# A float32 two-block transformer: last attention product, routing and experts joined in one block, routing by pairs of tiles

## The chip, the cores and the metric

The kernel runs on one core of a Trainium2 chip. The metric is the time of one execution in microseconds (us).

## The reference

512 tokens of width 1024 in float32 pass through a first model (pooling mixer, latent attention, two SwiGLU layers, a final norm) and then through a second block. Of the second block, what matters here is its end:

```
x = x + diff_attention(rmsnorm(x, norm_mix))        # its last step: o @ w_out
h = rmsnorm(x, norm_ffn)
logit_g = h @ w_group + b_group                     # 4 groups
g_sel   = argmax(logit_g);  gate_g = softmax(logit_g)[g_sel]
logit_e = (h @ w_router + b_router)[g_sel]          # the 4 experts of that group
top_v, top_i = top_k(softmax(logit_e), 2);  top_v = top_v / sum(top_v)
x = x + sum over the two experts e of gate_g * top_v[e] *
        (silu(h @ w_gate[e]) * (h @ w_up[e])) @ w_down[e]     # 16 experts, inner width 512
```

## The kernel before

X holds the 512 tokens as 4 tiles of 128 tokens on the partitions. Every large product is made as three matmuls of reduced-precision halves: `product` (L248 to L252) takes a high and a low half of both operands. The halves are made on the way: ScalarE (ACT) writes the high half, VectorE (DVE) subtracts it from the original. Weights stream in units of 128 x 2048 floats (1 MB), in the first part through `raw`, WH, WL, in the experts through `eraw` (8 slots), WEH, WEL (4 slots each).

`da_out` is the last attention product. PE turns the four tiles of heads (L1793), then makes 16 `unit_into` calls: 4 weight units times 4 tiles, each 12 matmuls with 512 columns. DVE adds each finished tile to X (L1884), ACT sums its squares into the junk space `da_flat` (L571). Then `recycle()` frees the semaphores behind a barrier of all engines, the memory of the attention is given back, and `run_experts` opens a new block. Only there do the loads of the first 8 expert units start (`prefetch`, L2171), because `eraw` lies where the attention's tiles were.

`route` follows in the order written out: root and reciprocal of the four sums (L265, L272); DVE makes the normed rows of all tiles with the gain (`rows_g`, L2037), PE turns them (L1962), ACT and DVE split them into halves (L2003, L2046), PE makes logits for all 512 tokens (24 matmuls of 512 columns), DVE copies them, PE turns them back (L1974). A chain of small DVE instructions then finds the group and the two experts by maxima and first matches (L2054 to L2076). PE counts how many earlier tokens chose each expert (`ranked`, L1979 and L1982), DVE works out a slot for each token and writes one-hot rows (L2086 to L2107), PE turns these into two tables, token and share of each slot, with 8 float32 matmuls (L1989). ACT copies the shares out, DVE the indices. SP, the queue that issues plain loads and stores, stores the normed rows in `moe_rows` and X in `out` meanwhile (L1951 to L1954), with the second four expert units behind them.

Then a loop runs over rounds of at most 128 tokens per expert (one round with these inputs) and inside it over the 16 experts. POOL gathers 128 rows of `moe_rows` by index (L2410, L2414), PE turns them (L2210), ACT and DVE split them (L2281, L2344), PE makes gate, up and down products from 6 units per expert, DVE making each unit's low half (L2339) after ACT's high half (L2277). ACT scales the result by the share (L2298), and POOL adds it to the rows of `out` (L2425). Each new expert unit is requested by SP when DVE is done with the unit in its slot (L2192). Gathered rows lie in X's first two tiles, results in its last two, so the loop may not start before X is stored.

## Time and profile before

| | us |
|---|---|
| median of three runs (lowest, highest) | 1587.02 (1586.5, 1595.58) |
| the profiled execution: its time, its span | 1586.74, 1584.7 |
| last attention product, from its first product matmul to the last, on the span's clock | 1186.7 to 1230.5 |
| first expert matmul | 1279.1 |
| ACT's scaling of the last expert's result | 1573.2 |

All starts are microseconds from the start of the span. The span is what the profiler saw of the program; the execution's own time is 2.0 us longer. PE is TensorE, PEld its loads of stationary operands, DVE VectorE, ACT ScalarE, POOL GpSimd, SPq the DMA issues of SyncE. A fp32 matmul whose operands are not in the reduced type leaves two records per instruction, a fp32 transpose one.

### The profile page before, as it was taken

To read this page: it belongs to the slowest core of one execution; us is meant where nothing else is said; L and a number is where in the kernel's file an instruction comes from. 1 tells how busy PE (TensorE), PEld (TensorE's weight loads), DVE (VectorE), ACT (ScalarE), POOL (GpSimd) and SP (SyncE) were. 2 spreads that over 40 slices of the span, in tenths; PEclk is the share of its full clock that TensorE was granted. 3 is DMA by queue.
4 is the path that set the end of the run, shared out by engine and by line. 5 is a ranking of instruction groups with operands and counts; after the bars stand their busy time and mean duration, and the time that the engine had idled before them with its cause. 6 is when DMAs were issued, how large, how long until landed. Compare 5 with 4: busy or idle time off the path is not lost. (4 is left out here: it accounts for less than half of the span.)

```text
span 1584.7 us, 18928 instructions
## 1 busy us (share of the span) xinstructions
PE 1505.3 (95%) x7353; PEld 1238.4 (78%) x7353; DVE 781.5 (49%) x922; ACT 674.1 (43%) x854; POOL 77.2 (5%) x57
## 2 busy tenths in 40 slices
PE   8999999999899999999999999999879479999996
PEld 7888888888787788888888887888558368888885
DVE  6432333222575334333332226344872578888884
ACT  5322222211356433322221125434861267777783
POOL 0000000000000000000000000000220012211110
PEclk9999999999999999999999999999989789999998
DMA  6222223223130112223233231322000889999993
GB/s 240 77 83 106 102 83 106 93 94 115 59 128 6 57 65 106 79 106 106 79 106 107 80 120 53 131 99 80 27 1 1 317 306 380 384 382 383 392 390 81
DMA packets 36160, 226.19 MB, mean 143 GB/s; under 512 B 5223, under 2 KB 5479, under 8 KB 11776
## 3 DMA queue, kind: packets, MB, share of 16 engines
q1 hardware_dynamic: 31344, 212.05, 35.4%
q0 software_dynamic: 4608, 13.22, 3.6%
q8 instruction: 45, 0.74, 0.2%
q14 instruction: 19, 0.16, 0.0%
q10 hardware_dynamic: 144, 0.03, 0.0%
HBM read 215.21 MB, written 13.63 MB: 144 GB/s over the span
## 5 line engine op out<-in xcount | busy, mean ns | idle before, releaser
L245 DVE TENSOR_TENSOR WL<-raw,WH 128x2048 fp32r<-128x2048 f32 x93 | 214.0, 2301 | 432.7 <-ACT WH L240 432.7
L250 PE MATMUL PS<-AH,WL 128*128 128x512 f32 (+1 forms) x768 | 286.4, 373 | 4.3 <-DVE AL L319 4.3
L251 PE MATMUL PS<-AL,WH 128*128 128x512 f32 (+1 forms) x768 | 285.8, 372 | 0.0
L252 PE MATMUL PS<-AH,WH 128*128 128x512 f32 (+1 forms) x768 | 285.7, 372 | 0.0
L240 ACT ACTIVATE WH<-raw 128x2048 fp32r<-128x2048 f32 x93 | 177.6, 1910 | 241.1 <-PE PS L252 241.1
L2339 DVE TENSOR_TENSOR WEL<-eraw,WEH 128x2048 fp32r<-128x2048 f32 x96 | 216.7, 2287 | 17.1 <-ACT WEH L2277 17.1
L2277 ACT ACTIVATE WEH<-eraw 128x2048 fp32r<-128x2048 f32 x96 | 181.6, 1912 | 19.8 <-PE PS L252 18.8
L250 PEld LDWEIGHTS PS<-AH,WL 128*128 128x128 f32 x768 | 145.4, 189 | 29.6 <-DVE AL L319 4.5
L252 PEld LDWEIGHTS PS<-AH,WH 128*128 128x128 f32 x768 | 145.3, 189 | 25.0
L251 PEld LDWEIGHTS PS<-AL,WH 128*128 128x128 f32 x768 | 145.4, 189 | 24.9
L250 PE MATMUL PS<-WH,AL 128*128 128x512 f32 (+2 forms) x416 | 155.3, 373 | 7.7 <-DVE WL L245 7.7
L252 PE MATMUL PS<-WH,AH 128*128 128x512 f32 (+2 forms) x416 | 153.2, 368 | 0.0
L251 PE MATMUL PS<-WL,AH 128*128 128x512 f32 (+2 forms) x416 | 153.1, 368 | 0.0
L250 PE MATMUL PS<-WEH,AH 128*128 128x512 f32 x256 | 103.5, 404 | 2.5 <-DVE AH L2344 2.5
L251 PE MATMUL PS<-WEL,AH 128*128 128x512 f32 x256 | 101.9, 398 | 0.0
L252 PE MATMUL PS<-WEH,AH 128*128 128x512 f32 x256 | 101.8, 398 | 0.0
L250 PEld LDWEIGHTS PS<-WH,AL 128*128 128x128 f32 x416 | 78.9, 190 | 21.8 <-DVE WL L245 6.8
L252 PEld LDWEIGHTS PS<-WH,AH 128*128 128x128 f32 x416 | 78.9, 190 | 12.7
L251 PEld LDWEIGHTS PS<-WL,AH 128*128 128x128 f32 x416 | 79.0, 190 | 11.9
L250 PE MATMUL PS<-WH,f0FL 128*128 128x512 f32 x176 | 69.8, 396 | 0.0
L252 PE MATMUL PS<-WH,f0FH 128*128 128x512 f32 x176 | 69.6, 396 | 0.0
L251 PE MATMUL PS<-WL,f0FH 128*128 128x512 f32 x176 | 69.6, 395 | 0.0
(312 smaller groups left out, 2104.2 us busy)
## 6 DMA issues: line engine op xcount, KB each, us to landing
eraw<-experts SPq DMA_DIRECT2D x96, 1024.0 KB, 12.8
raw<-stream SPq DMA_DIRECT2D x94, 1024.0 KB, 4.8
moe_rows<-moe_rows_g SPq DMA_DIRECT2D x5, 512.0 KB, 14.4
X<-x SPq DMA_DIRECT2D x4, 512.0 KB, 4.6
out<-X SPq DMA_DIRECT2D x1, 2048.0 KB, 20.3
ffn_row<-rows SPq DMA_DIRECT2D x2, 512.0 KB, 10.0
final_row<-rows SPq DMA_DIRECT2D x2, 512.0 KB, 6.2
cst<-consts SPq DMA_DIRECT2D x1, 733.5 KB, 13.3
```

Source lines behind the costliest of these rows:

```text
L240: act.activation(WH[:, u % SLOTS, :], raw[:, u % SLOTS, :], ACT.Copy).then_inc(unit_hi, 1)
L245: dve.tensor_tensor(WL[:, u % SLOTS, :], raw[:, u % SLOTS, :], WH[:, u % SLOTS, :].bitcast(F32), ALU.subtract).then_inc(unit_lo, 1)
L250: pe.matmul(acc, lhs_lo, rhs_hi, start=start, stop=False)
L251: pe.matmul(acc, lhs_hi, rhs_lo, start=False, stop=False)
L252: return pe.matmul(acc, lhs_hi, rhs_hi, start=False, stop=stop)
L2277: act.activation(WEH[:, k % ESLOTS, :], eraw[:, k % ERAW, :], ACT.Copy).then_inc(unit_hi, 1)
L2339: dve.tensor_tensor(WEL[:, k % ESLOTS, :], eraw[:, k % ERAW, :], WEH[:, k % ESLOTS, :].bitcast(F32), ALU.subtract).then_inc(unit_lo, 1)
```

## The change

One block now holds the attention's end, the routing and the experts: the barrier and the second block are gone. Three things allow it. The memory of `eraw` is laid over the attention's QT, KT, V and probabilities (for which the output O and the scratch `half` change places), and SP requests the first four expert units once all scores are made, the other four once the last head is weighted. X itself is turned and multiplied by router weights that carry the gain; the factor 1/root of a token is applied to its 20 logits afterwards. These logits are plain float32 matmuls with the turned X as stationary operand. And the tiles are routed in two pairs: the first pair between the units of the attention product, the second behind it.

Instead of the chain of maxima, an expert's rank within its group is counted: all 4 x 4 differences of a group are compared with a tiny constant and summed. The first table holds the tokens alone, as reduced-type matmuls in two parts; the shares have a table of their own behind it, and the exponentials stand next to it. The last tile is added, gained and turned in halves. In the expert loop, DVE copies index and share of the next round at the end of a round instead of at its beginning, and splits two units, not three, before the first rows.

```diff
...
-        differential_attention(block, later, w, v, down_made, mix_row_here, mix_row, mix_rows_g)
+        scored, weighed, made, heads_lo = differential_attention(block, later, w, v, down_made, mix_row_here, mix_row,
+                                                                 mix_rows_g)
+        later.close()
+        wctx.close()
+        m = expert_memory()
+        run_experts(block, m, *route(block, m, scored, weighed, made, heads_lo))
...
-    O = flat[:, 0:T * D].rearrange("p (t d) -> p t d", t=T)
-    half = flat[:, T * D:2 * T * D].rearrange("p (m n) -> p m n", m=2)
+    O = flat[:, T * D:2 * T * D].rearrange("p (t d) -> p t d", t=T)
+    half = flat[:, 0:T * D].rearrange("p (m n) -> p m n", m=2)
...
-        square_sums(act, added, sem("do_next_summed"), O, range(T))
...
+def expert_memory():
...
+    m.told_share = m.rows_g[:, 0, 0:512].rearrange("p (k n) -> p k n", n=ROUNDS * E)
+    sb("expert_gap", [P, SLOTS * UNIT - n[0] // 4])
+    m.WEL = sb("WEL", [P, ESLOTS, UNIT], F32R)
+    m.eraw = sb("eraw", [P, ERAW, UNIT])
+    with ExitStack() as before:
+        m.XT = sb("moe_turned", [P, T, C, P], where=before)
+    m.WEH = sb("WEH", [P, ESLOTS, UNIT], F32R)
...
+def route(block, m, qk_used, weighed, made, heads_lo):
...
+        sp.wait_ge(qk_used, 2 * H * T)
+        m.prefetch(sp, 0, 4)
+        sp.wait_ge(weighed, H * T)
+        m.prefetch(sp, 4, ERAW)
...
+        x_out(0)
+        sp.dma_start(out[S:S + P, :], X[:, 0, :]).then_inc(x_stored, 16)
+        x_out(1)
+        row_out(0)
+        sp.dma_start(moe_rows[S:S + P, :], m.rows_g[:, 0, :]).then_inc(rows_stored[0], 16)
+        row_out(1)
+        x_out(2)
+        row_out(2)
+        row_out(3)
+        x_out(3)
...
+        def turn_x(t, half):
+            pe.wait_ge(added, t + 1 + (half if t == last else 0))
+            for c in range(4 * half, 4 * half + 4):
+                mm = pe.transpose(PS[:, 2 * t + half, cols(c % 4)], X[:, t, cols(c)], ident)
+            mm.then_inc(x_turned, 1)
+
+        def logits(t, half):
+            if t == last and half:
+                pe.wait_ge(copied_last, 1)
+            else:
+                pe.wait_ge(copied, t + 1)
+            for c in range(4 * half, 4 * half + 4):
+                mm = pe.matmul(PS[:, 2 * t, 0:20], m.XT[:, t, c, :], m.wr[:, c, :],
+                               start=(c == 0), stop=(c == C - 1))
+            if half:
+                mm.then_inc(logits_made, 1)
+
...
+        unit_into(3, 0).then_inc(made, 1)
+        unit_into(3, 1).then_inc(made, 1)
+        turn_x(0, 0)
+        turn_x(0, 1)
+        unit_into(2, 2)
+        turn_x(1, 0)
+        turn_x(1, 1)
+        pe.wait_ge(weighted, 1)
+        logits(0, 0)
+        logits(0, 1)
+        unit_into(3, 2).then_inc(made, 1)
+        logits(1, 0)
+        logits(1, 1)
+        unit_into(2, last).then_inc(unit_used, 1)
+        pe.wait_ge(tables, 2)
+        pe.wait_ge(selected, 2)
+        pe.matmul(PS[:, 1, 0:2 * E], m.before_r[:, :], m.both[:, 0:2, :].rearrange("p t e -> p (t e)"),
+                  start=True, stop=False)
+        pe.matmul(PS[:, 1, E:2 * E], m.ones_r[:, :], m.both[:, 0, :], start=False, stop=True).then_inc(ranked, 1)
+        turn_x(2, 0)
+        turn_x(2, 1)
+        for half in range(2):
+            for j in (6, 7):
+                mm = unit_half(3, last, j, half)
+            mm.then_inc(unit_used if half else made, 1)
+        turn_x(last, 0)
+        turn_x(last, 1)
+        for t in (2, last):
+            logits(t, 0)
+            logits(t, 1)
+        table(0)
+
+        pe.wait_ge(selected, 3)
+        pe.matmul(PS[:, 5, 0:3 * E], m.before_r[:, :], m.both[:, 2:5, :].rearrange("p t e -> p (t e)"),
...
+        table(1).then_inc(tabled, 1)
+
+        pe.wait_ge(weighted_out, 1)
+        for n in range(2 * T):
+            k, t = divmod(n, T)
+            mm = pe.matmul(PS[:, 7, 0:ROUNDS * E], ALF[:, k, cols(t)], m.told_share[:, n, :],
+                           start=(n == 0), stop=(n == 2 * T - 1))
+        mm.then_inc(shares_tabled, 1)
...
+        for t in range(last):
+            square(t)
+            act.wait_ge(summed, t + 1)
+            root(t)
+            act.wait_ge(x_turned, 2 * t + 2)
+            act.activation(m.XT[:, t, :, :], tile_banks(t), ACT.Copy).then_inc(copied, 1)
+        square_half(0)
+        act.wait_ge(x_turned, 2 * last + 1)
+        act.activation(m.XT[:, last, 0:4, :], PS[:, 2 * last, :].rearrange("p (c s) -> p c s", s=P),
+                       ACT.Copy).then_inc(copied, 1)
+        square_half(1)
+        act.wait_ge(sum_added, 1)
+        root(last)
+        act.wait_ge(scaled, 2)
+        act.wait_ge(inverted, T)
+        act.activation(m.rows_g[:, last % 2, :], m.rows_g[:, last % 2, :], ACT.Copy,
+                       scale=rstd[:, last:T]).then_inc(gained, 1)
...
+            dve.wait_ge(step, n[0])
+            then(dve.tensor_tensor(D4, fours.unsqueeze(2).broadcast_to([P, 10, 4, 4]),
+                                   fours.unsqueeze(3).broadcast_to([P, 10, 4, 4]), ALU.subtract))
+            then(dve.tensor_tensor(D16, D16, const("order").unsqueeze(1).broadcast_to([P, 10, 16]), ALU.is_ge))
+            then(dve.tensor_reduce(m.rank[:, ts, :, :].rearrange("p t g e -> p (t g) e"), D4, AX_X, ALU.add))
+            then(dve.tensor_scalar(m.group[:, ts, :], m.rank[:, ts, 0, :], 0.0, None, ALU.is_equal))
+            group = m.group[:, ts, :].unsqueeze(3).broadcast_to([P, 2, G, 4])
+            dve.scalar_tensor_tensor(m.both[:, ts, :].rearrange("p t (g e) -> p t g e", g=G), m.rank[:, ts, 1:5, :],
+                                     1.5, group, ALU.is_lt, ALU.mult).then_inc(selected, 1)
+            for k in range(2):
...
+        invert(0)
+        row(0)
+        invert(1)
+        row(1)
+        add(2)
+        logit(0)
+        logit(1)
+        select(0)
+        invert(2)
+        row(2)
+        place(0)
+        add_half(0)
+        dve.wait_ge(rows_stored[1], 16)
+        gain_half(0)
+        add_half(1)
+        gain_half(1)
+        dve.wait_ge(x_turned, 2 * T)
+        dve.tensor_copy(m.XT[:, last, 4:8, :], PS[:, 2 * last + 1, :].rearrange("p (c s) -> p c s", s=P)
+                        ).then_inc(copied_last, 1)
+        dve.wait_ge(summed, T + 1)
+        dve.tensor_tensor(rstd[:, last:T], m.halves[:, 0:1], m.halves[:, 1:2], ALU.add).then_inc(sum_added, 1)
+        logit(2)
+        invert(last)
+        logit(last)
+        select(1)
+        then(dve.tensor_reduce(m.small[:, 0, :], m.L[:, :, 0:G], AX_X, ALU.max))
+        dve.tensor_tensor(m.group_less[:, :, :], m.L[:, :, 0:G],
+                          m.small[:, 0, :].unsqueeze(2).broadcast_to([P, T, G]), ALU.subtract).then_inc(exp_ready, 1)
...
+        dve.wait_ge(tabled, 1)
+        then(dve.tensor_scalar(m.nothing[:, :], PS[:, 3, 0:ROUNDS * E], 0.0, const("nobody"), ALU.is_equal,
+                               ALU.mult))
+        then(dve.scalar_tensor_tensor(m.slot_index[:, 0:ROUNDS, :].rearrange("p r e -> p (r e)"),
+                                      PS[:, 3, 0:ROUNDS * E], -1.0, m.nothing[:, :], ALU.add, ALU.add))
+        dve.tensor_copy(m.index[:, :], m.slot_index[:, 0, :]).then_inc(index_ready, 1)
...
+        for pair in range(2):
+            for k in range(2):
+                own = slice(T * k + 2 * pair, T * k + 2 * pair + 2)
+                at = slice(4 * pair + 2 * k, 4 * pair + 2 * k + 2)
+                ins = dve.tensor_tensor(m.told_share[:, own, :].rearrange("p k (r e) -> p k r e", e=E),
+                                        m.met[:, own, :].unsqueeze(2).broadcast_to([P, 2, ROUNDS, E]),
+                                        m.turn_of[:, at, :].unsqueeze(3).broadcast_to([P, 2, ROUNDS, E]), ALU.mult)
+        ins.then_inc(weighted_out, 1)
+        dve.wait_ge(shares_tabled, 1)
+        then(dve.tensor_copy(m.slot_share[:, 0:ROUNDS, :].rearrange("p r e -> p (r e)"), PS[:, 7, 0:ROUNDS * E]))
+        dve.tensor_copy(m.share_now[:, :], m.slot_share[:, 0, :]).then_inc(weight_ready, 1)
...
-                dve.wait_ge(indexed, 3)
-                dve.wait_ge(x_stored, 32)
-                dve.wait_ge(rows_stored, 16 * (T + 1))
...
...
+            dve.wait_ge(y_free, E * r + E + 2)
+            dve.tensor_copy(index[:, :], m.slot_index[:, bass.ds(r + 1, 1), :].rearrange("p r e -> p (r e)")
+                            ).then_inc(index_ready, 1)
+            dve.wait_ge(y_made, E * r + E + 1)
+            dve.tensor_copy(share[:, :], m.slot_share[:, bass.ds(r + 1, 1), :].rearrange("p r e -> p (r e)")
+                            ).then_inc(weight_ready, 1)
...
+        pool.wait_ge(x_stored, 16 * (T + 1))
+        pool.wait_ge(rows_stored[0], 48)
+        pool.wait_ge(rows_stored[1], 32)
...
-recycle()
-wctx.close()
-run_experts()
```

DVE, from the indices to the first splits. `expert_index` and `expert_share` are what POOL and ACT read, WEL<-eraw is the low half of an expert unit, AH<-PS that of gathered rows. Before:

```order
L2121 SCALAR_TENSOR_TENSOR slot_index<-PS,route_nothing 128x64
L2332 UNCONDITIONAL_BRANCH
L2180 TENSOR_LOAD counts
...
L2363 COPY expert_index<-slot_index 128x16
...
L2366 COPY expert_share<-slot_weight 128x16
...
L2339 TENSOR_TENSOR WEL<-eraw,WEH 128x2048
```

and now:

```order
L2244 COPY expert_index<-slot_index 128x16
L2246 TENSOR_TENSOR route_met<-route_chosen,route_logits 128x128
...
L2257 TENSOR_TENSOR route_met<-route_chosen,route_share 128x128
L2264 TENSOR_TENSOR moe_rows_g<-route_met,route_turn_of 128x128 x4
L2269 COPY slot_share<-PS 128x64
L2270 COPY expert_share<-slot_share 128x16
L2454 UNCONDITIONAL_BRANCH
L2302 TENSOR_LOAD expert_counts
...
L2461 TENSOR_TENSOR WEL<-eraw,WEH 128x2048
```

The index is written ahead of the read of the round count, and the whole making of the shares now stands between the index and the first split.

PE, behind the last product of the attention (the matmuls of `product` are left out). Before:

```order
L1962 MATMUL PS<-cst,moe_rows_g 128x128 x32
...
L1974 MATMUL PS<-cst,logits_turned 128x20 x4
L1979 MATMUL PS<-route_both,route_before 128x80
L1982 MATMUL PS<-route_both,ones_r 128x64
...
L1989 MATMUL PS<-route_told,route_onehot 128x128 x8
```

and now (L1973 turns X, L1982 makes logits, L1991 is the token table, L2052 the share table):

```order
L1973 MATMUL PS<-cst,X 128x128 x8
L1982 MATMUL PS<-router_weights,moe_turned 128x20 x16
L1991 MATMUL PS<-route_told,AL 128x64 x4
L2039 MATMUL PS<-route_both,route_before 128x48
L2044 MATMUL PS<-route_both,route_ones 128x48 x2
L2044 MATMUL PS<-route_both,route_ones 128x32
L2044 MATMUL PS<-route_both,route_ones 128x16
L1991 MATMUL PS<-route_told,AL 128x64 x4
L2052 MATMUL PS<-moe_rows_g,AL 128x64 x8
```

Three of four tiles' turns and half of the logits have moved ahead of these rows, between the product's units; the turning of the gathered rows comes only behind the share table.

## Rows read from the trace of the kernel before

**Rows 1.** Busy time by stretch: attention product, routing, expert phase
```profile
core 0: us, PE busy (x) PEld busy (x) DVE busy (x) ACT busy (x) POOL busy (x), PEclk, DMA share, GB/s
1200.00:1230.00 30.00, 30.00 (x134) 24.86 (x133) 8.14 (x5) 5.38 (x7) 0.00 (x0) 1.00 0.00 1
1230.00:1279.00 49.00, 19.60 (x92) 14.65 (x90) 31.30 (x76) 18.18 (x26) 3.11 (x3) 0.68 0.87 337
1320.00:1540.00 220.00, 220.00 (x1022) 179.09 (x1021) 192.94 (x110) 172.57 (x122) 44.74 (x23) 1.00 1.02 386
```

**Rows 2.** DVE's timeline, end of attention product: start, length, instruction, idle before it
```profile
1225.09 1.22 DVE L1884 TENSOR_TENSOR X<-X,PS 128x1024 f32<-128x1024 f32 x1 [4.22 <-PE PS L252]
1230.53 1.22 DVE L1884 TENSOR_TENSOR X<-X,PS 128x1024 f32<-128x1024 f32 x1 [4.22 <-PE PS L252]
```

**Rows 3.** Timeline of the routing, all engines
```profile
1249.67 0.42 PE L1974 MATMUL PS<-cst,logits_turned 20*128 20x20 f32 x4 [0.77 <-DVE logits_turned L2049]
...
1255.03 0.40 PE L1979 MATMUL PS<-route_both,route_before 128*128 128x80 f32 x1 [4.95 <-DVE route_both L2076]
...
1256.27 0.29 DVE L2086 TENSOR_TENSOR route_met<-route_chosen,PS 128x128 f32<-128x128 f32 x1 [0.70 <-PE PS L1982]
...
1257.66 0.69 DVE L2097 TENSOR_TENSOR route_entry<-route_chosen,route_turn_of 128x512 f32<-128x512 f32 x1
...
1259.60 1.65 DVE L2107 TENSOR_SCALAR route_onehot<-cst,route_slot 128x128 f32<-128x128 f32 x8
...
1261.30 3.79 PE L1989 MATMUL PS<-route_told,route_onehot 128*128 128x128 f32 x16 [5.07 <-DVE route_onehot L2107]
```

**Rows 4.** Timeline from the indices to the first expert matmul
```profile
1266.84 0.17 DVE L2363 COPY expert_index<-slot_index 128x16 uint32 x1 [1.17 <-ACT slot_weight L2011]
...
1268.03 1.14 POOL L2410 DMA_INDIRECT X<-moe_rows,expert_index  x1 [95.78 <-issue]
1268.55 7.31 ACT L2277 ACTIVATE WEH<-eraw 128x2048 fp32r<-128x2048 f32 x4 [1.05 <-issue]
...
1270.49 6.70 DVE L2339 TENSOR_TENSOR WEL<-eraw,WEH 128x2048 fp32r<-128x2048 f32 x3 [3.28 <-ACT WEH L2277]
...
1274.70 1.96 PE L2210 MATMUL PS<-cst,X 128*128 128x128 f32 x8 [9.62 <-DMA X<-moe_rows,expert_index]
1276.70 1.02 ACT L2281 ACTIVATE AH<-PS 128x1024 fp32r<-128x1024 f32 x1 [0.84 <-PE PS L2210]
...
1277.76 1.23 DVE L2344 TENSOR_TENSOR AH<-PS,AH 128x1024 fp32r<-128x1024 f32 x1 [0.57 <-ACT AH L2281]
...
1279.12 0.79 PE L250 MATMUL PS<-WEH,AH 128*128 128x512 f32 x1 [2.46 <-DVE AH L2344]
...
1286.20 1.04 PE L2210 MATMUL PS<-cst,X 128*128 128x128 f32 x8
```

**Rows 5.** Attention, full clock: float32 matmuls with two records each
```profile
1162.16 1.06 PE L1682 MATMUL PS<-da_V,d_turned_probs 128*128 128x128 f32 x8
```

**Rows 6.** The page: DMA issues, KB each, median us to landing
```profile
moe_rows<-moe_rows_g SPq DMA_DIRECT2D x5, 512.0 KB, 14.4
...
X<-x SPq DMA_DIRECT2D x4, 512.0 KB, 4.6
out<-X SPq DMA_DIRECT2D x1, 2048.0 KB, 20.3
```

**Rows 7.** Waits of the expert phase (1279 to 1585)
```profile
ACT WEH L2277 <- PE PS L252: 18.8, 30, 0.9
```

**Rows 8.** SP's requests of expert units: time to landing over the phase
```profile
DMA to landing us min/median/max: 4.8/12.6/17.7
```

**Rows 9.** Timeline of the end
```profile
1573.19 1.11 ACT L2298 ACTIVATE X<-PS,expert_share 128x1024 f32<-128x1024 f32 x1 [6.72 <-PE PS L252]
1575.10 1.55 POOL L2425 DMA_INDIRECT out<-X,expert_index  x1 [12.82 <-ACT X L2298]
```

945 lines of the change are left out of this document (457 added, 488 removed).

## The prediction

> **What bounds the kernel now.** I read the busy time by stretch first, then the timelines where PE's share falls, then the waits of the expert phase. PE is the bound nearly everywhere: it is busy all 30.0 us of the stretch in the attention product and all 220.0 us of the one in the expert phase, at full granted clock (1.00, 2.4 GHz) [rows 1]. The hole lies between: from 1230 to 1279 PE works 19.6 of 49.0 us and is granted 0.68 [rows 1]. The last product ends about 1230.4 (the last add starts at 1230.53 [rows 2]); the first expert matmul starts at 1279.12 [rows 4]. These 48.6 us are a chain in which one engine at a time works: last add, sum, barrier, normed rows, turns, halves, logits, selection, slots, table [rows 3], indices, gather, turn, halves [rows 4]. The change can only shorten this chain; the 16 experts behind it cost 294.1 us (1279.12 to 1573.19 [rows 4, 9]) and are not touched inside. Their waits show ACT waiting for PE, 18.8 us, not for a DMA [rows 7], so PE sets their pace. I therefore work out when the first expert matmul starts in the new kernel, on the same clock, and take the rest as it is.
>
> **What stays.** One `unit_into` takes half of the time between two adds, (1230.53 - 1225.09) / 2 = 2.72 us [rows 2]. The new code keeps the same 16 calls, so without insertions the last one ends at 1230.4.
>
> **Added among the units, on the path.** PE now also does, before its last unit is complete: turns of three tiles at 1.04 each (eight turns at full clock [rows 4]), 3.1; logits of two tiles; and the two count matmuls of the first pair, 0.5. A tile's logits are 8 float32 matmuls, 16 records; 8 such records with 128 columns took 1.06 [rows 5], so 0.13 each and 2.1 a tile. The trace has no such matmul with 20 columns against 128 x 128 stationary: the nearest bounds are 0.105 a record (4 in 0.42 [rows 3], small stationary operand) and 0.24 (16 in 3.79 at half clock [rows 3]). I take 0.13, since the row with the same stationary size says so at the clock that this stretch has. Two tiles: 4.2. Sum 7.8, last half unit done at 1238.2. This work is not lost: it was in the hole.
>
> DVE's share of the first pair (two rows of 1.2, selection, slots, third row) lies beside these units: all of place(0) should end about 1237.2, 1.1 before PE's last half unit. It is the thinnest cover here; each us by which DVE is later there delays the last add by as much.
>
> **From the last add to the logits.** Half an add and half a turn, 0.7 and 0.6 with hand-overs (halves of 1.22 [rows 2] and 1.04), to 1239.7. Tiles 2 and 3 then take 4.2 of logits: 1243.9. Removed by this are the barrier, the root of all tiles in one, 4.9 of rows, halving and turning back; the old logits were ready at 1250.1.
>
> **Selection.** After the logit's scaling (0.2), three DVE instructions over 160 elements and two small ones. Small ones take 0.17 [rows 4], 128 elements 0.29, 512 elements 0.69 [rows 3]; so 160 take 0.33, and each waits 0.04 for the one before. Sum 1.5 + 0.2: 1245.7. The old chain took from 1250.1 to 1255.0. Five count matmuls as before, from 1255.03 to DVE's read at 1256.27, 1.2 [rows 3]: 1247.0.
>
> **Slots and token table.** For one pair: products 0.4, sum 0.25, three or four small ones 0.8, told over 256 elements 0.42, four one-hots at 1.65 / 8 = 0.21 [rows 3]: 2.7, to 1249.7. The old one took 4.9 (1256.3 to 1261.2). Its table took 3.79; the second half of the token table is four reduced-type matmuls, 0.25 each like the count matmuls, with hand-over 1.1: 1250.8. Three DVE instructions later, at 1251.6, the index stands (old 1267.0 [rows 4]). That is 15.4 earlier.
>
> **Given back: the shares stand before the splits.** The order of DVE shows it. Products, sums and a difference 0.8; ACT's exponential 0.3; five instructions 1.1; four over 128 elements 1.2: at 1255.0 PE gets its share table, 8 float32 matmuls, 16 records. At half clock (PE has been nearly idle since 1244, as it was in the old hole at 0.68 [rows 1]) 16 took 3.79 [rows 3]; at full clock they would take 2.1 [rows 5]. I take 3.8: 1258.9; two copies 0.4: 1259.3. DVE then reads the round count: before, this read stood ahead of the index and showed as 1.17 idle; ACT's shows as 1.05 [rows 4]. I take 1.1, to 1260.4. Now two splits at 6.70 / 3 = 2.23, and the rows' low half 1.23 [rows 4]: 1266.1, first matmul 1266.3. Formerly DVE had made three splits while the gather was still under way.
>
> **Beside it, and not last.** POOL can gather 1.0 after the index (as 1267.0 to 1268.0 [rows 4]), 1252.6; 6.5 to the landing (1268.03 to 1274.7, in heavy traffic [rows 4]) gives 1259.2; PE is held by the share table and its own read of the count until 1260.0; turn 2.0, ACT 1.0: 1263.1, before DVE's second split ends. ACT has split three units by 1261. The requests of the 8 expert units go out in the attention and end before 1195, where the DMA engines were idle (share 0.00 from 1200 [rows 1]).
>
> The gather also waits for the last store of X, requested near 1244.0. The old 512 KB row stores took 14.4 to land and the 2 MB one 20.3, but behind 4 MB of expert units; a 512 KB load took 4.6 [rows 6]. I take 4.6, landing 1248.6, before the index. The Trainium skill, "DMA: Bandwidth & Descriptors", section "Anatomy of one DMA, SWDGE (gpsimd) path", gives a fixed 2.0 us plus bytes over 436 GB/s, a receipt from HBM being most of the fixed part; 512 KB would come to an estimated 3.2 us. By that rule the store hides too; by the 14.4 of the row it does not, and no row here shows a store on idle queues.
>
> **End.** The loop's end now holds DVE back for the last scatter and two copies: 0.2 each and their waits, 0.6 after the landing. Bounds: 0.4 to 1.2.
>
> **Sum.** 1266.3 - 1279.1 = -12.8, plus 0.6 = -12.2. On the profiled execution: 1586.7 - 12.2 = 1574.5; the median of the runs is 0.3 above that execution, so 1574.8. Bounds: logits at 0.105 a record -1.6, at half clock throughout +7.0; share table at full clock -1.7; count read and end -0.5 to +0.8. So 1571 to 1582.6.
>
> **Rivals.**
>
> A. Stores are slow. For it: 14.4 and 20.3 [rows 6]. Against it: nothing else is in the queues. At 14.4 the third tile's row, which waits for the first row's stores (requested 1223, DVE there at 1233.6), comes 3.8 late and the last add 3.3; the last store of X lands at 1261.7, gather 1262.7, landing 1269.2, then 4.4 as before (1274.7 to 1279.1): 1273.6, that is 7.3 later than forecast: 1582.1.
>
> B. The shares don't hold up DVE: PE is still at full clock for them and the count read is cheap. Then 1.7 + 0.7 less and the gather's side (1263.1 - 1.7) is not later: 1572.4. With gaps in my chain also smaller by a few tenths each the time would fall below 1571. For it: the token and count matmuls are near. Against: the old hole had 0.68.
>
> C. Half clock for the logits of tiles 2 and 3 and everything behind, because PE stops and starts from 1238 on: 32 records at 0.24 instead of 0.13, +3.5: 1578.3. For it: after 9.62 of idle, eight turns took 1.96 against 1.04 [rows 4]. Against: my gaps here are under 1 us.
>
> D. The other side: the DMA engines become the bound of the expert phase. They are at share 1.02 with 386 GB/s [rows 1], and the landing of a unit stretches from 4.8 to 17.7 us [rows 8]; a slot gives 8 units times 294.1 / 96 = 24.5, less about 4 for the splits' lead, so some 20. If the rate fell by 10% below 386 (for instance by where the moved `eraw` lies), landing would pass 20 and each expert take 18.4 x 1.1 = 20.2 instead of 18.4, + 1.84 x 16 = 29.4, net +17.2: 1604.2. It decides from a landing above 20. Against it: nothing in the phase changes in bytes or order, and ACT waits for no DMA now [rows 7].
>
> E. The change doesn't overlap: DVE's first pair runs past PE's units by more than its 1.1 of cover, for instance by the 2.7 of place(0): +1.6, 1576.4.
>
> **How the numbers follow.** Forecast 0.5, A 0.1, B 0.13, C 0.1, D 0.04, E 0.13. The range 1570.0 to 1582.0 takes in all but D, part of A and the low end of B. No change means within 1% (15.9 us), about what a measurement of this kernel can tell. Faster by more needs a time under 1571.1, the low part of B and of the forecast's spread: 0.17. Slower by more than 1% needs D: 0.03 of its 0.04. Within 1%: 0.80.
>
> **What would show it.** First expert matmul near 1266, DVE's first split near 1260 just behind `expert_share`, eight share-table matmuls of about 3.8 us in front of the gathered rows' turn, an index about 1251.6, X's last store landed before 1250, expert phase 294. Wrong would be: a DVE wait for stored rows before the third row, a gather that waits for stores, ACT waiting for landings in the expert phase, or PE waiting inside the units for halves or logits.

## The result, and the profile after

The changed kernel took 1573.74 us (median of 8 runs, 1570.04 to 1580.69), the kernel before, measured together with it, 1589.41 (8 runs). The ratio is 0.9902 with a 95% interval of 0.9879 to 0.9924: faster by 1.0%, just inside what was called no change. The forecast was 1574.8, in a range of 1570.0 to 1582.0. Measured twice more, each time beside the kernel before, the changed kernel gave 0.9892 [0.9865, 0.9918] and 0.9904 [0.9879, 0.9930], so about 1% in all three.

The profiled execution took 1572.86 us, its span 1571.0 (before: 1586.74 and 1584.7). To see where the 13.7 us of the span went, I cut both spans at three anchors. The first is in unchanged code, ACT's table load at the end of the attention's softmax; it started at 1173.00 before and here at:

```profile
1174.18 1.28 ACT L1782 ACT_TABLE_LOAD   x1
```

| stretch | before | after | difference |
|---|---|---|---|
| start of span to this table load | 1173.00 | 1174.18 | +1.2 |
| to the first expert matmul (1279.12, now 1266.48) | 106.12 | 92.30 | -13.8 |
| to ACT's scaling of the last result (1573.19, now 1559.93) | 294.07 | 293.45 | -0.6 |
| to the end of the span | 11.51 | 11.07 | -0.4 |

The first row is a drift of unchanged code; over the runs of this study the table load starts anywhere from 1172.65 to 1178.33. Everything below is therefore measured from an anchor inside the run. The last two rows are not clear of the scatter between runs: the third stretch takes 290.45 us in e1 and 293.20 in e12, both this same kernel, and the last one 11.07 to 11.65 in the changed kernel and the edits of it below. What is clear of it is the hole. Busy time by stretch, answering [rows 1] (columns: stretch, its length, then busy time and instructions of PE, PEld, DVE, ACT, POOL, the granted clock, DMA share, GB/s):

```profile
1200.00:1230.00 30.00, 30.00 (x152) 25.33 (x151) 10.36 (x12) 8.04 (x11) 0.00 (x0) 1.00 0.27 106
1230.00:1265.00 35.00, 22.76 (x126) 20.37 (x125) 23.83 (x84) 17.56 (x22) 4.19 (x3) 0.68 0.27 94
...
1306.00:1526.00 220.00, 219.06 (x1038) 180.98 (x1037) 193.36 (x110) 172.52 (x123) 44.88 (x23) 1.00 1.02 389
```

In the first row DVE and ACT do 10.36 and 8.04 us of work where they did 8.14 and 5.38, and PE is still full. The hole is 14 us shorter, and PE's granted clock in it is 0.68, as before. In the last row PE loses 0.94 of 220.00 us; it lost nothing there in the kernel before. The hole itself, in the timeline (start, length, instruction, idle before it and what ended it), answering [rows 3, 4]:

```profile
1236.82 0.86 DVE L2189 TENSOR_SCALAR AL<-cst,route_slot 128x128 fp32r<-128x128 f32 x4
...
1237.60 0.68 DVE L2123 TENSOR_TENSOR X<-X,PS 128x512 f32<-128x512 f32 x1
...
1238.38 0.69 DVE L2128 TENSOR_TENSOR moe_rows_g<-X,final_row 128x512 f32<-128x512 f32 x1
...
1238.99 0.68 DVE L2123 TENSOR_TENSOR X<-X,PS 128x512 f32<-128x512 f32 x1
...
1239.73 0.66 PE L1973 MATMUL PS<-cst,X 128*128 128x128 f32 x4 [0.74 <-DVE X L2123]
...
1240.23 4.76 PE L1982 MATMUL PS<-router_weights,moe_turned 128*128 128x20 f32 x32
...
1246.90 0.41 PE L2039 MATMUL PS<-route_both,route_before 128*128 128x48 f32 x1 [1.04 <-DVE route_both L2155]
...
1252.39 0.17 DVE L2244 COPY expert_index<-slot_index 128x16 uint32<-128x16 uint32 x1
...
1255.63 3.68 PE L2052 MATMUL PS<-moe_rows_g,AL 128*128 128x64 f32 x16 [3.86 <-DVE moe_rows_g L2264]
...
1259.10 1.92 PE L2332 MATMUL PS<-cst,X 128*128 128x128 f32 x8
1259.35 0.23 DVE L2269 COPY slot_share<-PS 128x64 f32<-128x64 f32 x1 [3.77 <-PE PS L2052]
...
1260.71 4.49 DVE L2461 TENSOR_TENSOR WEL<-eraw,WEH 128x2048 fp32r<-128x2048 f32 x2 [0.93 <-ACT WEH L2399]
...
1265.12 1.22 DVE L2466 TENSOR_TENSOR AH<-PS,AH 128x1024 fp32r<-128x1024 f32 x1
...
1266.48 0.79 PE L255 MATMUL PS<-WEH,AH 128*128 128x512 f32 x1 [5.46 <-DVE AH L2466]
```

Read it backwards. The first expert matmul (last row) waited for the rows' low half, that one stood behind two splits on DVE without an idle moment, the splits stood behind `slot_share`, and that waited 3.77 us for the share table on PE. The turn of the gathered rows (1259.10) has no idle before it, so the gather had landed already. The 0.93 put down to ACT is most likely the read of the round count, which stands there in DVE's order: ACT's WEH had been begun at 1256.07, its first unit done about 1258.

The stores, answering [rows 6] (page, DMA issues):

```profile
out<-X SPq DMA_DIRECT2D x5, 512.0 KB, 2.7
moe_rows<-moe_rows_g SPq DMA_DIRECT2D x5, 512.0 KB, 2.7
```

And two views of the expert phase, answering [rows 7, 8]: a wait (us in total, times, longest), and SP's requests of expert units:

```profile
ACT WEH L2399 <- DMA eraw<-experts: 24.5, 22, 2.9
```
```profile
DMA to landing us min/median/max: 4.8/16.5/21.9
```

ACT now waits for units to land, 22 times and 24.5 us in all, where it did not before; the landings are longer (4.8, 12.6, 17.7 before). In the stretch of 220 us above PE loses 0.94 beside it. Both differ between runs of this kernel: in e1 ACT waits 16.5 us and PE loses nothing of the same 220, in e12 18.5 and 0.77.

### The profile page after: what moved, and what is told of

It is laid out like the page before. It is cut to its first block, busy times and chain, and to the rows that moved or that the text cites. A ratio compares the mean times of both kernels' runs of the same rounds, so it can differ in the third digit from the quotient of the medians.

```text
span 1571.0 us, 19018 instructions
## 1 busy us (share of the span) xinstructions
PE 1505.6 (96%) x7399; PEld 1245.2 (79%) x7399; DVE 779.9 (50%) x941; ACT 674.1 (43%) x853; POOL 78.9 (5%) x57
## 4 chain that ended last, share of the span: by engine, by line
PE 53%; DVE 5%; DMA 3%; ACT 2%; issue 2%; DVEq 0%; ACTq 0%; SPq 0%; POOLq 0%
PE PS L255 16%; PE PS L257 16%; PE PS L256 16%; DMA eraw<-experts 3%; PE PS L1642 1%; PE PS L1662 1%; ACT WEH L2399 1%; PE PS L2332 1%; PE PS L1653 1%; DVE da_flat L1716 1%; DVE WL L250 1%; DVE WEL L2461 1%; PE PS L1982 1%; PE PS L1453 0%; PE PS L2355 0%
## 5 line engine op out<-in xcount | busy, mean ns | idle before, releaser
L2399 ACT ACTIVATE WEH<-eraw 128x2048 fp32r<-128x2048 f32 x96 | 182.4, 1915 | 35.1 <-DMA eraw<-experts 24.5
L256 PEld LDWEIGHTS PS<-AL,WH 128*128 128x128 f32 x768 | 145.6, 190 | 24.8
L256 PEld LDWEIGHTS PS<-WL,AH 128*128 128x128 f32 x416 | 79.3, 191 | 12.2
```

The source lines that it names most:

```text
L256: pe.matmul(acc, lhs_hi, rhs_lo, start=False, stop=False)
L2399: act.activation(WEH[:, k % ESLOTS, :], eraw[:, k % ERAW, :], ACT.Copy).then_inc(unit_hi, 1)
```

## The experiments

All are edits of the changed kernel, and all ratios are against the kernel before, measured beside them. e1 to e4 were measured together, e5 to e8 together, and e9 to e12 together.

The table load is not a good enough anchor for edits that are worth 1 to 3 us. Between it and the add of tile 1 the attention product begins, and this stretch takes 46.5 to 46.7 us in the first profile, e1 and e7 to e12, but 47.9 to 48.8 in e2 to e6: in the 10 us that begin 15 us behind the table load PE is granted 1.00 in the first profile, e1 and e12, and 0.84 to 0.94 in e2 to e6. Only e4's edit touches anything before that add (it takes away early requests), and e2, e3, e5 and e6 show the same shift without it, so it is no effect of the edits. The add of tile 1 stands behind that stretch and in front of all that the other edits move:

```profile
1220.90 1.22 DVE L2114 TENSOR_TENSOR X<-X,PS 128x1024 f32<-128x1024 f32 x1 [1.42 <-PE PS L257]
```

From there to the first expert matmul, in one profile each, with the 32 logits records of tiles 2 and 3 set apart, because their length changes from run to run without an edit that reaches them (3.65 in e6, 5.83 in e5):

| profile | add of tile 1 | to the first expert matmul | logits of tiles 2, 3 | the rest | against the changed kernel |
|---|---|---|---|---|---|
| changed kernel | 1220.90 | 45.58 | 4.76 | 40.82 | |
| e1_ctrl (the same kernel) | 1222.28 | 45.79 | 4.97 | 40.82 | 0.0 |
| e12_ctrl (the same kernel) | 1220.40 | 45.68 | 4.81 | 40.87 | 0.0 |
| e2_index_late | 1226.21 | 43.37 | 3.65 | 39.72 | -1.1 |
| e3_pairs_serial | 1223.85 | 54.45 | 6.86 | 47.59 | +6.8 |
| e4_prefetch_late | 1225.89 | 50.41 | 5.72 | 44.69 | +3.9 |
| e5_peel | 1225.95 | 43.66 | 5.83 | 37.83 | -3.0 |
| e6_share_r | 1221.51 | 42.71 | 3.65 | 39.06 | -1.8 |
| e7_warm | 1222.22 | 54.93 | 4.88 | 50.05 | +9.2 |
| e8_peel_warm | 1222.13 | 55.05 | 4.99 | 50.06 | +9.2 |
| e9_both | 1222.47 | 41.94 | 4.94 | 37.00 | -3.8 |
| e10_wide | 1219.33 | 41.88 | 4.87 | 37.01 | -3.8 |

**e1_ctrl**: the changed kernel as it is.

> The changed kernel once more, as the measure for the other three runs of this call. Ratio to the kernel before 0.990 (0.987 to 0.993). In its trace the expert phase, from the first expert matmul to the last scatter, 295 to 296 us, with ACT waiting up to some 25 us for landings of expert units, and the first expert matmul 92 us after the table load that ends the attention.

1574.71 us, ratio 0.9892 [0.9865, 0.9918]. The first expert matmul starts 92.30 us after the table load, as in the first profile; from the add of tile 1, without the logits, the same kernel repeats to 0.05 us, while the medians of such runs move by a us or two. The expert phase does not repeat like that: from the first expert matmul to the last scatter it took 292.36 us here, where 295 to 296 had been expected and the first profile had 295.36, and ACT waited 16.5 us for landings, not 24.5.

**e2_index_late**: the three instructions that make the index stand behind those of the shares.

```diff
-                dve.wait_ge(tabled, 1)
...
-                dve.tensor_copy(m.index[:, :], m.slot_index[:, 0, :]).then_inc(index_ready, 1)
...
                 ins.then_inc(weighted_out, 1)
+                dve.wait_ge(tabled, 1)
...
+                dve.tensor_copy(m.index[:, :], m.slot_index[:, 0, :]).then_inc(index_ready, 1)
```

> DVE makes the index behind the share entries, just before it waits for the share table, so the gather starts about 3 us later. Theory (DVE's splits behind the shares set the first expert matmul, the gather has about 2.5 us to spare): first expert matmul within -0.6 and +0.8 us of the changed kernel, time the same. Rival (the gather is what the table of tokens in front was for): +2.5 to +3.5 us.

1576.63 us, 0.9900 [0.9873, 0.9927], which the intervals don't separate from e1. From the end of the logits the index now takes 9.94 us, not 7.40, and PE waits for the gather:

```profile
1226.21 1.22 DVE L2114 TENSOR_TENSOR X<-X,PS 128x1024 f32<-128x1024 f32 x1 [1.42 <-PE PS L257]
...
1264.77 1.96 PE L2332 MATMUL PS<-cst,X 128*128 128x128 f32 x8 [2.36 <-DMA X<-moe_rows,expert_index]
...
1268.22 1.22 DVE L2466 TENSOR_TENSOR AH<-PS,AH 128x1024 fp32r<-128x1024 f32 x1
```

The low half (1268.22) has no idle before it: it follows the two splits, as the prediction had it, though ACT's high half was done only 0.4 us before. And it is not later but earlier: in the table above the first expert matmul comes 1.1 us sooner than in the changed kernel, outside the -0.6 to +0.8 expected. The reason stands in the same trace: with the index out of its way, DVE has the shares ready sooner, and PE begins the share table 9.51 us after the end of the logits instead of 10.62 (e1) and 10.64. So the "token table first" part of the change buys nothing at the end; it costs the 1.1 us by which it delays the shares. The median is too coarse to show this.

**e3_pairs_serial**: all units of the attention product first, then the turns, logits and counts of the first pair.

```diff
-                turn_x(0, 0)
-                turn_x(0, 1)
                 unit_into(2, 2)
-                turn_x(1, 0)
...
                 unit_into(3, 2).then_inc(made, 1)
-                logits(1, 0)
-                logits(1, 1)
                 unit_into(2, last).then_inc(unit_used, 1)
+                for half in range(2):
+                    for j in (6, 7):
+                        mm = unit_half(3, last, j, half)
+                    mm.then_inc(unit_used if half else made, 1)
+                turn_x(0, 0)
...
```

> PE makes all units of the attention product first and only then turns and multiplies tiles 0 and 1; everything else stays. Theory (the pairs gain only by DVE's work of the first pair, which then has no cover): last half add and first expert matmul 5 to 7 us later. Rival 1 (PE's 7.7 us of turns and logits were hidden by the order): 7.7 us or more. Rival 2 (the order is worth nothing, since PE does the same work): 0 to 1 us.

1584.94 us, 0.9955 [0.9932, 0.9977]: 10.2 us above e1, where 5 to 7 had been expected, and in the span of the first rival (7.7 or more). PE's timeline, with two rows of DVE:

```profile
1223.85 1.22 DVE L2114 TENSOR_TENSOR X<-X,PS 128x1024 f32<-128x1024 f32 x1 [1.41 <-PE PS L257]
...
1242.84 0.37 PE L2026 MATMUL PS<-route_both,route_before 128*128 128x32 f32 x1 [1.93 <-DVE route_both L2155]
...
1243.26 1.97 PE L1973 MATMUL PS<-cst,X 128*128 128x128 f32 x8
...
1246.93 0.68 DVE L2123 TENSOR_TENSOR X<-X,PS 128x512 f32<-128x512 f32 x1
...
1247.66 1.12 PE L1973 MATMUL PS<-cst,X 128*128 128x128 f32 x4 [2.43 <-DVE X L2123]
...
1249.96 6.86 PE L1982 MATMUL PS<-router_weights,moe_turned 128*128 128x20 f32 x32
```

From the add of tile 1 the first half add comes after 23.08 us, not 16.70: 6.4 later, within the 5 to 7, though PE's work before it is the same. The first pair's selection and slots, which lay beside the units, are now waited for (1.93, 2.43), since the last tile's add stands behind them on DVE. Behind it the turn of the last tile runs at half clock (0.4 more), and the 32 logits records take 6.86 in place of 4.76, another 2.1. The half clock is the term that I had left out. The first expert matmul comes 8.9 us later in all, logits included: that is what the order of the pairs is worth, more than half of the 13.8 us by which the hole is shorter. The rest of the 10.2 between the medians does not come from this stretch; in this profile the one before it is another 2.1 to 2.3 us longer, which no edit explains.

**e4_prefetch_late**: the first eight expert units are requested only when the last tile of X is complete, ahead of its stores.

```diff
-                sp.wait_ge(qk_used, 2 * H * T)
-                m.prefetch(sp, 0, 4)
-                sp.wait_ge(weighed, H * T)
-                m.prefetch(sp, 4, ERAW)
...
+                sp.wait_ge(added, T + 1)
+                m.prefetch(sp, 0, 4)
                 row_out(3)
                 x_out(3)
+                m.prefetch(sp, 4, ERAW)
```

> The first eight expert units are requested around the last stores, as in the kernel before, not in the attention. Theory (the early loading gains little by itself, since ACT reaches the first unit only at the end of routing; it keeps the stores and the gather quick): last store of X lands 10 us or more after its issue instead of 2.7, gather delayed, first expert matmul 0.5 to 4 us later. Rival (the early loading is most of the gain): 8 us or more later.

1577.78 us, 0.9897 [0.9869, 0.9924]; 3.1 above e1 by the medians, which the intervals don't separate. The profile separates it:

```profile
1225.89 1.22 DVE L2113 TENSOR_TENSOR X<-X,PS 128x1024 f32<-128x1024 f32 x1 [1.42 <-PE PS L257]
...
1271.87 1.97 PE L2331 MATMUL PS<-cst,X 128*128 128x128 f32 x8 [6.60 <-DMA X<-moe_rows,expert_index]
...
1274.93 1.22 DVE L2465 TENSOR_TENSOR AH<-PS,AH 128x1024 fp32r<-128x1024 f32 x1 [3.77 <-ACT AH L2402]
```

The stores queue behind units again (the last store of X lands after 11.7 us), the gather is issued 4.0 us after the index (1.2 in the changed kernel) and takes about 10 us to land, not 4.6. Without the logits, the first expert matmul comes 3.9 us later than in e1, within the 0.5 to 4 expected; the rival (8 us or more) is out. This is rival A's mechanism of the prediction, made on purpose: the early requests are what keeps it away.

**e5_peel**: high and low halves of the first two expert units are made while PE makes the share table; only the single round that these inputs have is handled.

```diff
+                for k in range(2):
+                    act.wait_ge(landed[k], 16)
+                    act.wait_ge(unit_used, k + 1)
+                    act.activation(WEH[:, k, :], eraw[:, k, :], ACT.Copy).then_inc(unit_hi, 1)
                 act.activation(spare[:, 5:6], ident[:, 0:1], ACT.Silu).then_inc(table_loaded, 1)
...
                 ins.then_inc(weighted_out, 1)
+                for k in range(2):
+                    dve.wait_ge(m.unit_hi, k + 1)
+                    dve.tensor_tensor(m.WEL[:, k, :], m.eraw[:, k, :], m.WEH[:, k, :].bitcast(F32),
+                                      ALU.subtract).then_inc(m.unit_lo, 1)
...
-                    lo(0)
-                    lo(1)
                     rows_out(0)
```

> ACT makes the high halves of expert units 0 and 1 ahead of its Silu table load, and DVE their low halves between the share entries and the wait for the share table; the loop no longer makes them (so it computes only the single round that these inputs have). Theory (DVE's two splits behind the share table set the first expert matmul, 4.5 us of them lie after the wait): first expert matmul 2.5 to 3.5 us earlier than in the changed kernel, time down by as much. Rival (PE's share table, the turn of the gathered rows and their halves are as late): 0 to 1 us.

1573.93 us, 0.9886 [0.9863, 0.9910]. The splits have left the path: DVE waits 1.78 us before the low half, for ACT.

```profile
1265.24 1.92 PE L2338 MATMUL PS<-cst,X 128*128 128x128 f32 x8
1267.19 1.02 ACT L2413 ACTIVATE AH<-PS 128x1024 fp32r<-128x1024 f32 x1 [2.42 <-PE PS L2338]
...
1268.24 1.23 DVE L2474 TENSOR_TENSOR AH<-PS,AH 128x1024 fp32r<-128x1024 f32 x1 [1.78 <-ACT AH L2413]
```

From the first half add to the first expert matmul it takes 26.92 us; the changed kernel took 28.88. That is 2.0 (3.0 if the logits, 1.07 longer in this run, are set aside, within the 2.5 to 3.5 expected), and the next limit is at once PE: share table, then turn. In the median it doesn't show.

**e6_share_r**: the shares' table in the reduced type, 8 records in place of 16; the shares are rounded to it.

```diff
-                    mm = pe.matmul(PS[:, 7, 0:ROUNDS * E], ALF[:, k, cols(t)], m.told_share[:, n, :],
+                    mm = pe.matmul(PS[:, 7, 0:ROUNDS * E], AL[:, k, cols(t)], m.told_share[:, n, :],
```

> The share table is made of reduced-type matmuls (8 records instead of 16), its entries rounded to that type and kept in a place of their own. Theory: DVE's wait for it falls from 3.8 us to 2.1 and everything behind comes 1.5 to 1.9 us earlier, since the table's length stands on the path one for one. Rival (the gather's side is as late): 0 to 0.5 us, DVE then waiting before the first rows' low half.

1573.05 us, 0.9896 [0.9870, 0.9922].

```profile
1255.14 1.91 PE L2053 MATMUL PS<-route_told_share,AL 128*128 128x64 f32 x8 [3.85 <-DVE route_told_share L2265]
1257.09 0.22 DVE L2270 COPY slot_share<-PS 128x64 f32<-128x64 f32 x1 [2.01 <-PE PS L2053]
1257.63 1.96 PE L2333 MATMUL PS<-cst,X 128*128 128x128 f32 x8 [0.58 <-DMA X<-moe_rows,expert_index]
```

DVE's wait falls from 3.77 to 2.01, and 25.97 us lie between the anchors of e5: 2.9 less than in the changed kernel, of which the logits (3.65 us) are 1.1 and the table 1.8. With e2 and e5 this shows the path of the changed kernel: shares, share table, two splits, low half. Each of the three edits shortened it, by 1.1, 3.0 and 1.8 us.

**e7_warm** and **e8_peel_warm**: discarded matmuls with 128 columns in PE's waits, to have the full clock back for the share table and the first products; e8 adds them to e5. There are 108: 8 before the counts, 22 before the second part of the token table, 34 before the share table and 44 behind the turn of the rows; the cut shows the first and the third group.

```diff
+                for _ in range(8):
+                    pe.matmul(PS[:, 2, 0:P], m.before_r[:, :], m.ones_r[:, :], start=True, stop=True)
                 pe.wait_ge(selected, 3)
...
                 table(1).then_inc(tabled, 1)
+                for _ in range(34):
+                    pe.matmul(PS[:, 2, 0:P], m.before_r[:, :], m.ones_r[:, :], start=True, stop=True)
```

> PE fills its waits from the first table to the first expert matmul with 108 matmuls of 128 columns into an unused PSUM bank. Theory (PE works at half clock here because it idles): granted clock near 1.00 up to the first expert matmul, share table 2.1 us instead of 3.7, first six expert matmuls at 0.23 instead of 0.43; together 3 to 4 us less. Rival (the clock falls for another reason, or comes back too late): no change of the share table, time the same or up to 1 us longer.

> Both of the edits before. Theory: the first takes away the two splits, the second shortens table, turn and first matmuls, so they add: 5.5 to 7 us less than the changed kernel, ratio to the kernel before 0.985. Rival (one hides the other's gain): no better than the better of the two.

1582.92 us, 0.9945 [0.9923, 0.9967], and 1581.68, 0.9944 [0.9923, 0.9965]: e8 is 7.8 us above e5, and e7 by its ratio some 6.5 to 8.5 us above the changed kernel. The theory of e7 and its rival (at most 1 us longer) both missed; for e8 its rival (one hides the other's gain) held. e7, by stretch and in PE's timeline:

```profile
1250.00:1270.00 20.00, 20.00 (x96) 20.00 (x95) 8.85 (x38) 9.09 (x8) 3.24 (x3) 0.50 0.17 54
```
```profile
1255.46 7.49 PE L2053 MATMUL PS<-route_ones,route_before 128*128 128x128 f32 x34
1262.75 3.62 PE L2058 MATMUL PS<-moe_rows_g,AL 128*128 128x64 f32 x16
```

PE is busy for all of 20.00 us, and granted 0.50 throughout. The theory fell: the clock did not come back, and at half clock each discarded matmul takes 0.22 us, so they outlast the waits that they were to fill. The 22 delay the index by 2.4 us against e1 (80.61 and 78.21 after the table load), the 34 hold the share table until 1262.8, 3.3 us after DVE has the shares ready, and the 44 take 9.63 us and end 3.8 us after the rows' low half is done. In e8 they end at the same place, 1277.2, though the low half is 3.0 us earlier than in e7: what e5 gains is hidden behind them.

**e9_both**: e5 and e6 together.

> The two edits of e5_peel and e6_share_r together, without any added matmul (it handles the single round of these inputs only, and rounds the share entries to the reduced type). Theory (the stretch behind the token table is a chain of DVE's shares, PE's share table, PE's turn of the gathered rows, one high and one low half, with the splits of the first two expert units now beside the routing): e5 showed the rows' low half 1.0 behind the end of PE's turn, so 8 share matmuls of 1.9 instead of 3.7 shorten the whole by another 1.8. First half add to first expert matmul about 24.5 to 25.5 us against 28.9 in the changed kernel, time 3 to 4.5 us below that of the changed kernel in this call. Rival (the gather's landing becomes what PE's turn waits for): PE's turn shows an idle that ends with the gather, and the gain stays at 2 us or under.

1571.27 us, 0.9885 [0.9860, 0.9909]. Between the anchors 25.20 us (1239.21 to 1264.41), within the 24.5 to 25.5 expected, against 28.93 in e12. The two edits are worth 3.0 and 1.8 alone and 3.8 together, and the rival shows its edge: PE's turn waited 0.52 for the gather. The median is only 1.7 below e12, not the 3 to 4.5 expected, in which the drift of the start (the table load at 1175.95, 2.3 later than in e12) may have a part; the intervals don't separate them.

**e10_wide**: e9 with six discarded matmuls of 512 columns in front of the share table and six behind the turn of the rows.

```diff
                 table(1).then_inc(tabled, 1)
+                for _ in range(6):
+                    pe.matmul(PS[:, 2, :], m.before_r[:, :], AL[:, 0, :], start=True, stop=True)
...
                     turn_rows(0)
+                    for _ in range(6):
+                        pe.matmul(PS[:, 2, :], m.before_r[:, :], AL[:, 0, :], start=True, stop=True)
                     gate(0, 0)
```

> e9_both plus 12 discarded reduced-type matmuls with 512 columns, six while PE waits for the shares and six while it waits for the first rows' halves. e7 and e8 tried matmuls with 128 columns, each with a load of its own, and the granted clock stayed at 0.50. Theory W (wide matmuls bring the clock back, as the expert products do some 3 to 4 us into their phase): six at half clock take 2.6 us and fit into the wait; then the share table or at least the rows' turn and the first products run at full clock, about 1 to 3 us less than e9_both. Rival N (they do not, within the 5 us that they fill): granted clock 0.50 to some 4 us into the expert products as before, and the time equal to e9_both or up to 2 us longer.

1566.73 us (6 runs, 1565.72 to 1570.54), ratio 0.9865 [0.9842, 0.9889]: the fastest kernel of the study. PE's timeline of e10, then the same place in e9:

```profile
1254.23 1.91 PE L2058 MATMUL PS<-route_told_share,AL 128*128 128x64 f32 x8 [1.15 <-DVE route_told_share L2270]
1256.68 1.97 PE L2341 MATMUL PS<-cst,X 128*128 128x128 f32 x8 [0.54 <-DMA X<-moe_rows,expert_index]
1258.30 2.91 PE L2382 MATMUL PS<-AL,route_before 128*128 128x512 f32 x6
1261.21 0.55 PE L255 MATMUL PS<-WEH,AH 128*128 128x512 f32 x1
1261.59 0.39 PE L256 MATMUL PS<-WEL,AH 128*128 128x512 f32 x1
...
1266.81 1.03 PE L2341 MATMUL PS<-cst,X 128*128 128x128 f32 x8
```
```profile
1264.41 0.79 PE L255 MATMUL PS<-WEH,AH 128*128 128x512 f32 x1 [2.59 <-DVE AH L2475]
1265.00 0.63 PE L256 MATMUL PS<-WEL,AH 128*128 128x512 f32 x1
...
1267.56 0.52 PE L256 MATMUL PS<-WEL,AH 128*128 128x512 f32 x1
1267.91 0.40 PE L257 MATMUL PS<-WEH,AH 128*128 128x512 f32 x1
...
1271.60 1.04 PE L2339 MATMUL PS<-cst,X 128*128 128x128 f32 x8
```

In e9 the expert products begin at half clock and take 0.63 each until 1267.6, 3.2 us in. In e10 the discarded six take that stretch upon themselves, inside a wait of 2.6 us, and all but the first product run at 0.39. The six in front of the share table brought nothing: it still took 1.91, and the turn behind it 1.97. The first product comes 25.14 us after the half add (e9: 25.20). From it to the turn of the next rows, the last row of each view, PE needs 5.60 us against 7.19, and 6.94 to 7.62 in all other profiles here: 1.6 us are this mechanism, within the 1 to 3 expected. Up to the end of the span nothing can be claimed: e10 takes 302.6 us from its first product, e9 304.0, but e1, the changed kernel without any of this, 301.8. So 1.6 of the 4.5 us between the medians of e10 and e9 are explained; the rest is not. Against e12, e10 has 3.8 less to the first product by the anchors and this 1.6 behind it, 5.4 of the 6.2 between those medians.

**e11_more_dma**: one more load of 1 MB for each eight expert units, into a place that nothing reads.

```diff
+                    sp.wait_ge(unit_lo, ERAW * i + 1)
+                    sp.wait_ge(extra_here, 16 * i + 16)
+                    sp.dma_start(m.rows_g[:, :, :].rearrange("p a d -> p (a d)"), stream[0, :, :]).then_inc(extra_here, 16)
                     for j in range(ERAW):
```

> The changed kernel with one more load of 1 MB per slot of eight expert units, into a place that nothing reads any more (12 extra loads in all, so 13% more bytes in the expert phase). Rival D of the prediction, as its price (the phase is already so near to the DMA engines' limit that more bytes stretch it one for one): share 1.02 at 389 GB/s leaves no reserve, 12 MB more at 389 GB/s are 32 us, of which the slack that the landings still have takes some; ACT's waits for units grow to many times the 24.5 us of now, time 15 to 32 us longer than the changed kernel. Theory (PE sets the pace with real slack behind it): time within 3 us, landing longer, ACT's waits for PE shrink.

1598.32 us, ratio 1.0052 [1.0032, 1.0072], 25.3 us above e12. By stretch, then the wait and the landings of the expert units, as above:

```profile
1306.00:1526.00 220.00, 208.47 (x953) 169.82 (x951) 176.59 (x100) 155.79 (x110) 43.09 (x22) 0.97 1.02 395
```
```profile
ACT WEH L2403 <- DMA eraw<-experts: 57.0, 37, 4.7
```
```profile
DMA to landing us min/median/max: 4.7/21.0/24.8
```

The loop has 11 passes and not the 12 that the expectation names, so 11.5 MB were added; at the 0.390 MB/us of the changed kernel's stretch they take an estimated 29.6 us. Paid are 25.3 by the medians and 23.1 from the first expert matmul to ACT's last scaling (316.28 us against 293.20 in e12). So the expert phase of the changed kernel is an estimated 4 to 7 us from being bound by the DMA engines: rival D's price was nearly right, its condition wasn't met. Not all that was paid is waiting. PE has holes of 11.5 us in 220, and its granted clock there is 0.97, not 1.00; over the whole phase its 1336 records keep it busy 9.0 us longer than in e12 (297.16 against 288.16). The sign to watch is the landing of the units, 21.0 in the median and 24.8 at most, against medians of 16.5, 14.8 and 15.3 and maxima of 21.9, 21.0 and 22.4 in the changed kernel's three profiles (first, e1, e12). The prediction's mark of 20 fits the median and not the maximum.

**e12_ctrl**: the changed kernel once more.

> The changed kernel once more, to be compared with e9_both, e10_wide and e11_more_dma on one chip. Every theory: ratio to the kernel before 0.989 to 0.991.

1572.98 us, 0.9904 [0.9879, 0.9930]; ACT waited 18.5 us for units, in 17 waits.

## Why the prediction was right, step by step

The mechanism was right and the total has some luck in it. The span moved by -13.7 us against -12.2 forecast, the errors of its terms pulling both ways. That the median came within 1.1 us of the forecast owes something to the kernel before, whose median moved from 1587.02 (three runs) to 1589.41 (eight): the medians measured together are 15.7 apart.

Starts as forecast, and as measured less the 1.2 us of drift, on the clock of the kernel before:

| step | forecast | measured |
|---|---|---|
| last half unit done | 1238.2 | 1237.1 |
| last half tile turned | 1239.7 | 1239.2 |
| logits ready | 1243.9 | 1243.8 |
| selection ready | 1245.7 | 1245.6 |
| counts read | 1247.0 | 1247.0 |
| slots' one-hots | 1249.7 | 1249.5 |
| index stands | 1251.6 | 1251.4 |
| PE gets its share table | 1255.0 | 1254.4 |
| share table done | 1258.9 | 1258.1 |
| DVE's first split | 1260.4 | 1259.5 |
| first expert matmul | 1266.3 | 1265.3 |

- **The chain held**, with every hand-over of the table within 1.1 us of where it was put. The first expert matmul moved by -13.8 against -12.8 forecast. 0.4 of the 1.0 came between the index and the share table, where the small instructions overlap by more than the row-by-row prices allowed.
- **Logits at 0.13 a record**: eight matmuls of a tile took 1.86 for 16 records at full clock, 0.116 each. The price from the nearest row was 0.014 too high. But the 32 records of tiles 2 and 3 took 4.76, so 0.149: in their course the clock falls. That is rival C in part (6.86 in e3 is nearly all of it, 3.65 in e2 and e6 none), worth 1.1 us here and different in nearly every run. The two errors cancel within 0.6 us: 4.2 forecast, 4.76 measured.
- **DVE's "thinnest cover"** was crossed. Its one-hots end at 1237.68, before PE's last half unit (1238.3) but 0.8 after the first one, and the second half add stands behind the gain of the first half (1238.38), which the forecast left out. It starts 0.7 after PE was done. So rival E's mechanism was there, with 0.7 and not 1.6 us, paid by PE being 1.1 earlier than forecast.
- **The shares hold DVE**: share table 3.68 at half clock (3.8 forecast), DVE's wait for it 3.77, count read 0.93 (1.1 forecast). Rival B fell by the clock: 3.68 for 16 records is the row of half clock, not of full. e6, with half as many records, takes 1.8 off the table and off the path.
- **The gather hides**: it landed after 4.3 to 4.9 us instead of the 6.5 taken from heavy traffic. In e2 it starts 2.5 us later behind the logits, and the low half still follows the splits without idle.
- **The stores hide**: 2.7 us each, where I took 4.6 and kept 14.4 as a rival. The Trainium skill's rule ("DMA: Bandwidth & Descriptors", section "Anatomy of one DMA, SWDGE (gpsimd) path", an estimated 3.2) was the nearer price for idle queues, 0.5 too high, though it is stated for the gpsimd path and SP issues these stores; e4 shows what the busy queue makes of it.
- **End**: forecast +0.6 for the two copies behind the last scatter. They stand at 1568.01 and 1568.14, 2.9 us before the span's end, and from the last scatter's issue to that end it took 9.2 us against 9.6 before. The forecast's 0.6 is not there: from ACT's last scaling to the end, forecast at 12.1, no profile here takes more than 11.65. DVE's copies lie beside the landing of the scatter, as the rest of the end does.
- **Expert phase** "taken as it is": -0.6, less than it varies by itself (290.45 in e1). The sentence that its waits would not change was wrong, and here the prediction's own sign of being wrong came true: ACT waits for landings, 16.5 to 24.5 us in the three profiles of the kernel, and the longest landings passed the 20 us of rival D. That this costs PE under 1 us of the 220 fits the 4 to 7 us of reserve that e11 gives. Why the landings became longer, with the same bytes in the same order, was not tried.

What makes most of the gain is the first pair beside the product's units: without that, the first expert matmul comes 8.9 us later (e3). The early requests of the expert units stand for 3.9 (e4), which may overlap with other parts of the change; the table's order costs 1.1 (e2). The counting of ranks in place of maxima, the logits' new form and the missing barrier were not tried one by one.

## What to carry to other kernels

When a stretch is a chain in which one engine at a time works, price the step that hands its work to an engine that is otherwise full: with the same work on PE, routing's first half between the units of the attention product made the first expert matmul 8.9 us earlier than behind them (e3), because its small instructions on DVE then came for nothing. Then walk the new chain from its end and ask which hand-over comes last. What feeds another branch (here the index) should not stand in front of it: it looked urgent, and moving it back gained 1.1 us (e2, one profile). Measure from an anchor close to the edit, and set apart what changes by itself: from the add of tile 1 to the first expert matmul this kernel repeats to 0.05 us without the logits, while the stretch before it moves by 2 us, the expert phase by 3 and the medians by 2, which hid e2, e5, e6 and half of e9.

## What the runs showed of the hardware

- The granted clock fell towards 0.50 (1.2 GHz) while PE was busy without a gap on matmuls with 20 columns. In the changed kernel this stretch reads 0.75 and the next 5 us 0.50; the same 32 records took 3.65 us in e2 and e6, 6.86 in e3:

```profile
1240.00:1245.00 5.00, 5.00 (x37) 5.00 (x36) 1.47 (x5) 3.17 (x6) 0.00 (x0) 0.75 0.10 40
```

- It stayed at 0.50 through 20.00 us in which PE was busy without a gap, mostly on matmuls with 128 columns (e7), and through the 7.00 us behind them. It rose 3.2 us into the expert products in e9 (512 columns), and about 3 us into the six discarded ones in e10, but not within the 2.9 us of the six before the share table. In this stretch, a PE that is busy without a gap was no sign of the full clock; only the granted clock of the row tells.
- With 20 columns a float32 matmul took as long as the load of its stationary operand: in the 32 records PEld is busy 4.75 of 4.76 us.

```profile
1240.12 4.75 PEld L1982 LDWEIGHTS PS<-router_weights,moe_turned 128*128 128x128 f32 x32
```

- A 512 KB store took 2.6 to 3.6 us on idle queues, against 14.4 behind expert units [rows 6].
- At a DMA share of 1.02 the phase was still bound by PE, with an estimated 4 to 7 us of 293 to spare; 11.5 MB more cost 25.3 us. The share does not tell the two cases apart (1.02 in both). PE's busy time does (219.06 against 208.47 of 220), and so do the landings of the units (median 21.0 against 14.8 to 16.5).
